# One transformer layer on one core: projections as three fp32r passes over an input kept in two parts

## What is computed

```python
mod = jax.nn.silu(c) @ p['w_ada'] + p['b_ada']
sh_a, sc_a, gt_a, sh_f, sc_f, gt_f = [m[:, None, :] for m in jnp.split(mod, 6, axis=-1)]
h = _rms_norm(x, p['g_pre_mix']) * (1.0 + sc_a) + sh_a
proj = h @ p['w_in']
q, k, v, xl, yl, ga, gr = jnp.split(proj, [o1, o2, o3, o4, o5, o6], axis=-1)
...
xc, conv_new = _causal_conv(xl, conv_prev, p['w_conv'], p['b_conv'])
hl, h_new = _rg_lru(xc, h_prev, ...)
o_lru = (hl * jax.nn.gelu(yl.astype(jnp.float32))).astype(x.dtype)
b_attn = o_attn @ p['w_attn_branch']
b_lru = o_lru @ p['w_lru_branch']
merged = jax.nn.sigmoid(ga) * b_attn + jax.nn.sigmoid(gr) * b_lru
x = x + gt_a * _rms_norm(merged @ p['w_out'], p['g_post_mix'])
h2 = _rms_norm(x, p['g_pre_ffn']) * (1.0 + sc_f) + sh_f
x = x + gt_f * _rms_norm(_hier_moe(h2, ...), p['g_post_ffn'])
```

## Time and profile before

| | us |
|---|---|
| median of three runs | 1967.49 (1965.16 to 1968.57) |
| the profiled execution, its own time | 1967.22 |
| its span, first to last instruction | 1965.4 |
| TensorE busy | 1766.9 |
| VectorE busy | 1277.9 |
| ScalarE busy | 1034.6 |
| mean granted TensorE clock | 0.954 of full speed |

### The profile page before, as it was taken

The page is one execution under the profiler, slowest core; times in us unless marked ns, Lnnn a source line. Parts: engine busy times, 40 slices in busy tenths (PEclk is TensorE's granted clock), DMA queues, the critical chain, the costliest instruction groups (busy, mean ns, idle before and its releaser), DMA issues.

```text
span 1965.4 us, 24197 instructions
## 1 busy us (share of the span) xinstructions
PE 1766.9 (90%) x8882; PEld 1395.4 (71%) x8882; DVE 1277.9 (65%) x1632; ACT 1034.6 (53%) x1414; POOL 305.7 (16%) x308
## 2 busy tenths in 40 slices
PE   3799987999999989999999997399999999999980
PEld 0566645666666679999999895277788878887860
DVE  4302236777787774454645655688888988988954
ACT  2413324545555463343544533277777877877744
POOL 0000001222222100000000200012323333332311
PEclk9899988999999999999999998599999999999995
DMA  9463230111111055364555546379999989899829
GB/s 357 172 243 118 75 91 4 36 46 47 47 47 44 30 211 201 119 225 125 179 184 185 179 169 251 133 274 371 368 378 394 367 349 378 359 363 373 344 115 264
DMA packets 93046, 403.69 MB, mean 205 GB/s; under 512 B 15255, under 2 KB 39991, under 8 KB 76568
## 3 DMA queue, kind: packets, MB, share of 16 engines
q1 hardware_dynamic: 75904, 375.41, 50.7%
q0 software_dynamic: 11904, 22.05, 3.6%
q10 hardware_dynamic: 5160, 5.18, 0.8%
HBM read 375.66 MB, written 46.81 MB: 215 GB/s over the span
## 4 chain that ended last, share of the span: by engine, by line
PE 65%; DVE 15%; DMA 10%; ACT 4%; issue 4%; SPq 1%; ACTq 0%; POOLq 0%; DVEq 0%; POOL 0%
PE ps L1657 62%; DMA wg<-w_gate 7%; DVE wd_low L1583 2%; DMA fy<-y_dram 2%; DVE wg_low L1583 1%; ACT wg_up L1061 1%; PE ps L1797 1%; DVE olst L1303 1%; DVE mx L1252 1%; DVE xc L1275 1%; PE ps L1987 1%; PE ps L1955 1%; DMA nsink<-sinks 1%; DMA wraw<-w_ga 1%; DVE xc L1294 1%
## 5 line engine op out<-in xcount | busy, mean ns | idle before, releaser
L924 ACT ACTIVATE wup<-wraw 128x1024 fp32r<-128x1024 f32 x120 | 126.6, 1058 | 252.5 <-PE ps L1657 231.9
L1358 DVE TENSOR_TENSOR wlow<-wraw,wup 128x1024 fp32r<-128x1024 f32 x120 | 146.5, 1224 | 151.7 <-ACT wup L924 151.2
L1657 PE MATMUL ps<-hT,wA 128*128 128x352 f32 x624 | 195.7, 470 | 12.2 <-ACT hT L781 12.0
L1657 PE MATMUL ps<-hT,wB 128*128 128x352 f32 x624 | 189.2, 459 | 0.5 <-ACT gB L868 0.5
L1583 DVE TENSOR_TENSOR wg_low<-wg,wg_up 128x2048 fp32r<-128x2048 f32 x68 | 152.8, 2289 | 43.7 <-ACT wg_up L1061 43.7
L1657 PEld LDWEIGHTS ps<-hT,wA 128*128 128x128 f32 x624 | 120.3, 195 | 81.4 <-ACT hT L781 12.3
L1583 DVE TENSOR_TENSOR wu_low<-wu,wu_up 128x2048 fp32r<-128x2048 f32 x68 | 155.6, 2289 | 15.8 <-ACT wu_up L1066 15.8
L1657 PEld LDWEIGHTS ps<-hT,wB 128*128 128x128 f32 x624 | 118.4, 190 | 64.1 <-issue 1.9
L1583 DVE TENSOR_TENSOR wd_low<-wd,wd_up 128x2048 fp32r<-128x2048 f32 x68 | 152.7, 2287 | 12.4 <-ACT wd_up L1071 12.3
L1061 ACT ACTIVATE wg_up<-wg 128x2048 fp32r<-128x2048 f32 x68 | 126.5, 1908 | 39.6 <-DMA wg<-w_gate 39.6
L1066 ACT ACTIVATE wu_up<-wu 128x2048 fp32r<-128x2048 f32 x68 | 130.0, 1913 | 23.3 <-PE ps L1657 23.2
(11 more groups left out here) (319 smaller groups left out, 4120.5 us busy)
## 6 DMA issues: line engine op xcount, KB each, us to landing
wg<-w_gate SPq DMA_DIRECT2D x34, 2048.0 KB, 12.8
wu<-w_up SPq DMA_DIRECT2D x34, 2048.0 KB, 13.7
wd<-w_down SPq DMA_DIRECT2D x34, 2048.0 KB, 8.2
wada<-w_ada SPq DMA_DIRECT2D x12, 2048.0 KB, 10.1
wraw<-w_ga SPq DMA_DIRECT2D x24, 512.0 KB, 3.9
wraw<-w_gr SPq DMA_DIRECT2D x24, 512.0 KB, 3.6
wraw<-w_at SPq DMA_DIRECT2D x24, 512.0 KB, 3.7
wraw<-w_lr SPq DMA_DIRECT2D x24, 512.0 KB, 3.5
```

Source lines behind the costliest of these rows:

```text
L924: act.activation(wup[n % UP][:, :, :], wraw[n % RAW][:, :, :], ACT.Copy).then_inc(w_rounded, 1)
L1358: V.tensor_tensor(wlow[n % RAW][:, :, :], wraw[n % RAW][:, :, :], wup[n % UP][:, :, :].bitcast(F32), ALU.subtract).then_inc(w_split, 1)
L1657: return pe.matmul(out, lhsT, rhs, start=start, stop=stop, skip_group_check=True)
```

## The change

Every projection is computed as three fp32r passes. For this:

- h is kept as hp_up (rounded, in memory of its own) and hp_low (what remains, in hT's place). VectorE's `split_h` makes one chunk's low part after ScalarE's shift has written the rounded one. Both parts are stored to DRAM (two stores of 4,224 KB where there was one), and the mixing stage loads both (`load_h`), so ScalarE and VectorE no longer round and split h there.
- Each weight tile of wA and wB, and wV, is rounded by ScalarE (`round_pair`) and split by VectorE (`split_pair`) before TensorE uses it. The table `PAIR` numbers these in the order in which ScalarE does them. The low part replaces the raw tile.
- The two key chunks are summed input chunk by input chunk into six PSUM banks, so TensorE starts once the first chunk of h is split.
- w_ada's second and third parts come in 16 pieces of 1,024 KB through one buffer, wlate, in place of 8 loads of 2,048 KB through two; `AFTER` says after which query chunk which piece is multiplied.
- In the rounds GpSimd copies the queries half by half in place of a product with halves, and no longer copies the values; ScalarE makes every second pT copy; the gelu's polynomial loses one VectorE instruction.
- The last yl chunk goes input chunk by input chunk too; the first weights of the mixing stage lie in hp_up's memory, so their loads wait for it (h_free).
- x after the mixing stage is stored to x1_dram, loaded back near the end (x1f), added by VectorE, and y is stored plainly from SP's queue.

```diff
+AFTER = {2: (5,), 3: (6,), 4: (7,), 5: (8,), 6: (9, 10), 7: (11,), 8: (12, 13), 9: (14, 15)}
...
+def pair_order():
+
+    order = [(0, 1), (1, 1), (2, 1), (0, 2)] + [((m + 1) % 2, (m + 1) // 2 + 1) for m in range(2, 10)] + [(1, 6), (0, 7), (0, 8)]
+    for i in range(2, KC):
+        order += [(1, 5 + i)] + ([(0, 7 + i)] if i + 1 < KC else [])
+    return order + [(1, 5 + KC)]
...
+            def ada_piece(n):
+
+                g, k = 1 + n // KC, n % KC
+                sp.wait_ge(ada_done, n + 1)
+                sp.dma_start(wlate[:, :], I["w_ada"][k * P:(k + 1) * P, 2048 * g:2048 * (g + 1)]).then_inc(ld_wada[0], 16)
...
-            sp.dma_start(h_dram[:, :, :], hT[:, :, :]).then_inc(st_h, 16)
...
+            sp.dma_start(hp_dram[0][:, :, :], hp_up[:, :, :].bitcast(F32)).then_inc(st_h, 16)
+            sp.dma_start(hp_dram[1][:, :, :], hp_low[:, :, :].bitcast(F32)).then_inc(st_h, 16)
+            for m in range(2, 10):
+                sp.wait_ge(proj_done, 3 * m + 3)
...
+                sp.dma_start(w[:, :, :], src).then_inc(ld, 16)
+                for n in AFTER[m]:
+                    if n + 1 < 2 * KC:
+                        ada_piece(n + 1)
...
-            load_source(0, 0, h_raw, h_dram)
...
             sp.wait_ge(u_out, 4 + KC * BLKS)
+            load_h(0)
...
+            for n in range(RAW - 1):
+                load_weights(STEPS[n])
             sp.wait_ge(proj_done, N_PROJ)
...
+            def round_pair(b, n):
+
+                ld, raw, up = ((ld_wA, wA, wA_up[n >= 7]), (ld_wB, wB, wB_up[(n > 1) + (n >= 6)]))[b]
+                act.wait_ge(ld, 16 * n)
+                act.activation(up[:, :, :], raw[:, :, :], ACT.Copy).then_inc(p_rounded, 1)
...
+                    if s == 1 and i >= 2:
+                        round_pair(1, 5 + i)
+                    if s == 3 and i == 0:
+                        round_pair(1, 6)
+                    if s == 6 and i + 1 < KC:
+                        round_pair(0, 7 + i)
...
+                    if 1 <= s <= KC and s % 2 == 0:
+                        act.wait_ge(u_turned, 8 * i + s - 1 + 3)
+                        act.wait_ge(u_pv, 8 * i + s - 1 + 1)
+                        act.activation(pT[:, 1, :, :], ps[:, 6, :].rearrange("p (k q) -> p k q", k=4), ACT.Copy).then_inc(u_kept_a, 1)
...
+            def split_pair(b, n):
...
+                dve.wait_ge(p_rounded, PAIR[b, n])
+                V.tensor_tensor(low[:, :, :], raw[:, :, :], up[:, :, :].bitcast(F32), ALU.subtract).then_inc(p_split, 1)
...
+                V.tensor_tensor(fy[0:n, t, 1, :], fy[0:n, t, 0, :], x1f[0:n, t, :], ALU.add).then_inc(y_added, 1)
...
+            def three(out, w, low, x, x_low, first, last):
+
+                mm(out, w, x, first, False)
+                mm(out, w, x_low, False, False)
+                return mm(out, low, x, False, last)
...
+            ada_piece(0)
+            ada_piece(1)
...
+            for m in range(2, 10):
+                up, low = ((wA_up[0], wA_low), (wB_up[1], wB_low))[m % 2]
+                pe.wait_ge(p_split, PAIR[m % 2, m // 2 + 1])
+                for g in range(GRP):
+                    pe.wait_ge(proj_kept, 3 * m + g - 2)
+                    project(ps[:, g, 0:GW], up, low, g).then_inc(proj_done, 1)
+                    if g == 1 and len(AFTER[m]) > 1:
+                        ada_piece(AFTER[m][0])
+                ada_piece(AFTER[m][-1])
```

More of the change, by code:

```diff
@@ L81 @@
 SOURCES = {"ga": 0, "gr": 0, "at": 1, "lr": 2}
+def pair_order():
[3 more added lines that the diff above has]
+    return order + [(1, 5 + KC)]
+PAIR = {key: n + 1 for n, key in enumerate(pair_order())}
 class Chain:
@@ L461, in ada_rows @@
                              ).then_inc(ld_wada[slot], 16)
-            for q in range(4):
+            for q in range(3):
                 ada_rows(0, q, q)
@@ new lines, in _ @@
+            split_pair(1, 1)
+            dve.wait_ge(ld_bada, 16)
+            dve.wait_ge(ada_done, 1)
+            V.tensor_tensor(modq[:, 0, :], ps[:, 3, :], badaq[:, 0, :], ALU.add).then_inc(ada_kept, 1)
+            dve.wait_ge(setup_pe, 2)
+            turned_mod = ps[:, 7, :].rearrange("p (c j r) -> p j c r", c=4, j=4)
+            for j in range(2):
+                c(V.tensor_copy(shT[:, 4 * j:4 * j + 4, :], turned_mod[:, j, :, 0:1 + NB]))
+                c(V.scalar_tensor_tensor(scT[:, 4 * j:4 * j + 4, :], turned_mod[:, 2 + j, :, 0:1 + NB], 1.0,
+                                         bc(gpre[:, 4 * j:4 * j + 4].unsqueeze(2), (P, 4, 1 + NB)), ALU.add, ALU.mult))
@@ new lines, in _ @@
+            scale_h(0)
+            dve.wait_ge(hs_stage, 1)
+            dve.wait_ge(hs_stage, 2)
+            V.tensor_tensor(hp_low[:, :, SEQ:TOK], hT[:, :, SEQ:TOK], hp_up[:, :, SEQ:TOK].bitcast(F32), ALU.subtract).then_inc(hs_stage, 1)
+            for k in range(1, KC):
+                scale_h(k)
+                dve.wait_ge(h_scaled, k)
+                split_h(k - 1)
+            dve.wait_ge(h_scaled, KC)
+            split_h(KC - 1)
+            dve.wait_ge(p_rounded, PAIR[2, 1])
+            V.tensor_tensor(wV_low[:, :, :], wV[:, :, :], wV_up[:, :, :].bitcast(F32), ALU.subtract).then_inc(p_split, 1)
@@ L1203, in _ @@
                 rope(p, kT[:, p, P:])
-            keep_mod(1)
-            with dve.Fori(0, 4) as i:
-                c.enter(i, 4)
-                for q in range(2):
-                    rope(2 * i + 2 + q, oT[:, bass.ds(2 * i + q, 1), :].rearrange("p a t -> p (a t)"))
-            c.leave(4)
+                if p == 0:
+                    split_pair(0, 2)
+            for m in range(2, 10):
+                split_pair((m + 1) % 2, (m + 1) // 2 + 1)
+                if m == 7:
+                    keep_mod(1)
+                rope(m, oT[:, m - 2, :])
             keep_mod(2)
@@ L1682, in _ @@
             ins.then_inc(setup_pe, 1)
-            ada(0, 2, 2, 1)
-            ada(0, 3, 3, 1).then_inc(ada_done, 1)
+            pe.wait_ge(setup_dve, 1)
+            for k in range(KC):
+                if k % 2 == 0 or k == KC - 1:
+                    pe.wait_ge(ld_wada[k // 2 if k < KC - 1 else 4], 16)
+                ins = ada(0, k, wada[k // 2][:, k % 2, :])
+            ins.then_inc(ada_done, 1)
             pe.wait_ge(ld_small, 16 * N_SMALL)
@@ L1734, in outs @@
                     if o < 6:
[L1735 to L1736 removed]
+                        up, low = (wA_up[i >= 1], wA_low) if o < 3 else (wB_up[2], wB_low)
+                        project(out, up, low, o % 3).then_inc(proj_done, 1)
                     else:
```

402 lines of the change are left out of this document (219 added, 183 removed).

## The result

The changed kernel takes 2031.86 us (median of four runs, 2028.35 to 2037.06), the kernel before 1967.41 in the same runs: ratio 1.0331, 95% interval 1.0302 to 1.036. It is slower by 64 us.

What follows compares the result with a forecast made beforehand. TensorE, 90% busy, was taken to bound the kernel, except VectorE in steps 3 to 7 of a round. Terms -3.7 + 58 - 4 (round 7) + 1 - 4 = +47.3 on about 1967 us gave 2015 us, range 1992 to 2034.

Steps and rivals of the forecast that it cites:

- A pass: TensorE projections: one pass at 352 columns costs 0.161 us, 72 of them 11.6 us, 2.7 us less a chunk.
- The rival that passes don't pay: TensorE projections: a pass costs 0.199 us, so nothing is freed and the total is above 2034 us; chance 1%.
- the estimate by a quarter of an fp32 product: TensorE projections, skill's four-pass rule: three passes cost 10.8 us a chunk, so 26 chunks free 94 us, not 70.
- The start: Key projections: first product at 51.0 instead of 59.15 us, -8; keys take 23.2 us plus 2.35 for low clock.
- w_ada through one buffer: Up to first sample scores: 32 us of waits and 5 to 7 of low clock against gains; -3.7, bounds -35 and +9.
- The rounds: Rounds 1 to 6: ScalarE's step 6 rounding waits for w_xl; +8 in round 1, +10 in each other, sum +58.
- Into mixing: From rounds to mixing: first product about 3.5 us later, mostly given back later in the stage; +1, bounds -1 and +4.
- The end: Final weighed sums and store: last sum at 1958, plain store over at 1961.5; -4 us, bounds -6 and -1.
- The rival of a hidden wait: Rounds, step 6: w_xl lands in time, TensorE gains 2.7 us in each of seven rounds, total 1942 us; chance 7%.
- the reading that a shorter product gives little in steps 3 to 7: Rounds: VectorE's nearly gapless chain bounds steps 3 to 7; shorter products count fully only in steps 0 to 2.
- The clock stays down: Rounds: TensorE's clock stays low for the round after each stall, 5 us more a round, about 2045 us; chance 12%.

Runs made afterwards that it cites:

- run 9: Kernel with all five moves together (1900.3 us) plus a fourth product, low by low, per input chunk in the 8 query chunks: 1929.2 us.
- run 4: Changed kernel plus 48 unused filler products on TensorE after the yl sum of step 7 in rounds 1 to 6: 2028.92 us.
- Run 5: Changed kernel with the two stores of h moved behind the load of w_xl[1] at the start of the rounds: 2015.57 us.
- run 6: Changed kernel with the second w_ada piece's load issued mid-chunk in the three query chunks with two pieces: 2011.92 us.
- run 1: Changed kernel with the load of w_xl[i+1] issued at step 2, ahead of the wait for step 7's yl sum: 1950.76 us.
- Run 7: Changed kernel with the first four mixing weights loaded right behind h, ahead of the attention output and two last stores: 2026.36 us.
- Run 10: Kernel with all five moves together (1900.3 us) plus a fourth product, low by low, in the rounds' 15 xl and yl chunks: 1941.42 us.

## Why the forecast was right, point by point

I forecast 2015 us and slower, with 1992 to 2034; it is 2031.9. The mechanism and its place are as forecast. The total is short by 17 us; of the 22 us by which the profiled execution lies above the sum of the terms, 5 are this execution's distance from the median. Two terms were too small, w_ada and the way into mixing, and the rounds were 3 us too large.

- **A pass.** Forecast 0.161 us at 352 columns. Products start 0.16 apart, and run 9 puts it to use: of 8 chunks x 24 x 0.161 = 31 us added, 30 appear in its trace, where 0.199 would have made 38. The rival that passes don't pay is out; so is the estimate by a quarter of an fp32 product, which would be 0.149.
- **The start.** Forecast 51.0 for the first product, measured 52.33. Keys forecast at 25.5 us, measured 25.35 (52.33 to the last end at 77.68).
- **w_ada through one buffer.** This term failed in size: forecast -3.7 up to the sample scores, measured +9.2 (268.19 against 259.01) in this execution and about +8 in four other versions with the same program up to there (266.7 to 267.2; a fifth, run 4, has 264.2). Its own parts, 32 of waits and 6 of clock against 46 of gains, add up to -8 and not to -3.7, a slip of 4 us that happened to bring the forecast nearer. So the parts miss by 16. The four waits behind chunk ends are 6.3 to 6.55 where I had 6.1. Piece 3 doesn't wait (I had 1.6 to 3.3). But piece 6 waits 12.76, not 5.9: the two stores of 4.2 MB hold back the load of wA for m = 4 and then the piece, and I had counted only what stuck out beyond wA's own slack. The second store landed at 151, the load of wA for m = 4 at 152.5, the piece at 155. Run 5 shows it. The waits come to 38.9 us in all, 6 or 7 more than forecast. The next part is the clock: runs 5 and 6 give about 2 us behind each wait, about 10 in all for five waits where I took 5 to 7. The rest, some 6 us, are gains that I had counted and that didn't come: 1.3 at the first product, and part of the swaps, for which TensorE's rows of before show nothing to win but the 3.03 us of waiting for qs; no run parts it further. My own upper bound for the term was +9. The reading of the earlier trace rows was off too: 19.0 and 18.2 are times from issue, and wA was issued 0.5 us behind the store, so it landed 1.3 us behind it and not 0.8. The order is as I read it.
- **The rounds.** Forecast +10 a round, measured +9.3. Its three parts, each by its own rows: the turn of step 7 later by 13.2 (forecast 13.2; t + 14.55 against t + 14.6 forecast), the rest of the round shorter by 5.4 (forecast 5.1; 50.5 before, 45.1 in run 1), and what is lost beside the wait, net, +1.55 (forecast 2, for the clock). Round 1 alone was forecast at +8 and is +8.1 (59.8 us between wB issues, 51.6 before). The rounds, from the first masks to the last issue of wB, give +50.7; forecast 54.
- **Into mixing.** The second term that failed: forecast +1, at most +4, measured +7.8 at the first product and +10.5 behind the stage. I had the bytes right (h in two parts, the attention output and two stores ahead of w_ga) but put the first product only 3.5 us later and let the saved splits of h pay for it. The wait is 9.92, and the stage gives nothing back. Run 7 shows that the order of the queue makes 8.6 of the wait, of which 5.5 count in the time and most of the remainder goes to the two waits that come in behind.
- **The end.** Forecast -4, measured -2.8 in the profile. The last sum is ready 37.95 us behind the first weighed sum, where I had 35.65; 1.73 of this is the wait for ScalarE at the second weighed sum. The last store takes 2.35 us, where I had 3.5. No run parts it further.
- **The rival of a hidden wait** was computed at 1942, from a gain of 2.7 a round. Run 1, which hides it, gives 1950.8, with a gain of 4.4 a round (51.9 to 47.5). So I had undervalued what shorter products bring beyond steps 0 to 2 in the rival, though not in the forecast. Run 10 looks at it from the other side: 5.5 of 7.7 us of added work count, and the rest fits into TensorE's idle time in the round. So the reading that a shorter product gives little in steps 3 to 7, because VectorE bounds them, was too strong. The total of this rival comes out near its number because its too small gain and its too favourable start offset each other.
- **The clock stays down**: no. In the changed kernel it is 0.60 in 453 to 457 and 1.00 from 457 on. These windows have the columns of run 4's:

```profile
449.00:453.00 4.00, 0.94 (x7) 0.50 0.00 0
453.00:457.00 4.00, 4.00 (x17) 0.60 0.02 6
457.00:461.00 4.00, 3.95 (x23) 1.00 0.00 0
```

The Trainium skill, "TensorE: Matmul & The Clock Gate", section "HAM oscillation — how this bites in real kernels", describes a kernel in which each stretch of matmuls after a wait for DMA starts at the slow clock: the trace agrees (0.50 up to 453), and run 1 puts the net price here at 1.55 us for a wait of 13.

What stays open: the 6 us of gains that didn't come before the sample scores, why the mixing stage beyond its first product loses 2.7 us more, and the part of the end.

## What to carry to other kernels

Before an engine is given a new instruction that waits for a load, find where that load stands in its queue and what the queue waits for ahead of it. A tile that was in time for its old user can be 12 us late for a new one, and then everything behind the new instruction on that engine is late too. Two cures were measured: issue the load when its buffer comes free (81 us back), or put the waiting instruction behind the urgent ones (67 us back, with the load still late). The same reading found the rest: a large store ahead of a load that is due soon, a one-buffer chain with a second load behind a chunk's end, weights behind data that is needed after them. With these moved, and w_ada's pieces 1 to 4 among the values, the change that cost 3.3% gained 3.5%.

## What was unexpected of the hardware

- The gains of the moves added: four measured alone come to 122.8 us, and together with a fifth that was estimated at 8 they gave 131.6, though TensorE is busy 90% of the time in that version (1700.4 of 1899.1 us).
- 48 products put into a wait of 10 us didn't keep the clock up to the end of the stall: two waits of 1.96 and 3.53 us came behind them, the clock stood at 0.50 from 444 to 450 all the same, and the time didn't change measurably.
- A landing of 512 KB takes 3.9 us when it is first in a burst and 6.8 as the fourth of it, behind a load and two stores of 512 to 528 KB each; alone, in run 1, it takes 3.5.
